# Attention logits: the product with the keys' low half on 64 rows for each map, two maps in two banks, no copy of that low half

## The reference, cut to what matters

```
q = q.reshape(bsz, s, B_HEADS, 2, B_HEAD_DIM) * ATTN_SCALE      # B_HEAD_DIM = 64
k = k.reshape(bsz, s, B_HEADS, 2, B_HEAD_DIM)
...
logits = jnp.einsum('bqhmd,bkhmd->bmhqk', qblk, k).astype(jnp.float32) + bias[None, None]
p = jax.nn.softmax(logits, axis=-1)
attn = p[:, 0] - lam * p[:, 1]
return jnp.einsum('bhqk,bkhd->bqhd', attn.astype(v.dtype), v)
```

## Time and profile before

| | |
|---|---|
| median of 3 runs | 1683.22 us (1682.72 to 1686.58) |
| the profiled execution's own time | 1683.37 us |
| its span in the trace | 1681.6 us |
| granted TensorE clock, mean | 0.999 |
| PE busy | 1673.0 us, 99% of the span |
| DVE, ACT, POOL busy | 1004.9, 832.6 and 805.6 us (60%, 50%, 48%) |

### The profile page before, as it was taken

The page is one execution under the profiler, slowest core; times in us unless marked ns, Lnnn a source line. Parts: engine busy times, 40 slices in busy tenths (PEclk is TensorE's granted clock), DMA queues, the critical chain, the costliest instruction groups (busy, mean ns, idle before and its releaser), DMA issues.

```text
span 1681.6 us, 24045 instructions
## 1 busy us (share of the span) xinstructions
PE 1673.0 (99%) x8873; PEld 1445.6 (86%) x8873; DVE 1004.9 (60%) x1640; ACT 832.6 (50%) x1509; POOL 805.6 (48%) x808
## 2 busy tenths in 40 slices
PE   9999999999999999999999999999999999999998
PEld 7888888888888899988888888888888888999886
DVE  4778876533338967661246788755333489666642
ACT  4676754222245566662255667432223555667322
POOL 3444332433354788854344334334333547888432
PEclk9999999999999999999999999999999999999999
DMA  7422223233333333342352222322342423333422
GB/s 253 136 76 76 76 97 105 75 100 112 129 135 100 101 101 101 102 162 94 97 197 82 94 76 76 101 97 78 100 150 85 142 98 101 101 101 101 163 95 82
DMA packets 147319, 182.77 MB, mean 109 GB/s; under 512 B 3040, under 2 KB 130706, under 8 KB 146194
## 3 DMA queue, kind: packets, MB, share of 16 engines
q1 hardware_dynamic: 147090, 181.35, 32.6%
q10 hardware_dynamic: 128, 0.09, 0.0%
HBM read 170.92 MB, written 10.50 MB: 108 GB/s over the span
## 4 chain that ended last, share of the span: by engine, by line
PE 98%; ACT 0%; DVE 0%; POOL 0%; issue 0%; ACTq 0%; POOLq 0%
PE banks L1852 19%; PE banks L1853 19%; PE banks L1854 19%; PE banks L2088 6%; PE banks L2093 5%; PE banks L2089 5%; PE banks L1887 3%; PE banks L1888 3%; PE banks L1889 3%; PE banks L2167 2%; PE banks L2169 2%; PE banks L2168 2%; PE banks L1916 2%; PE banks L1943 2%; PE banks L2018 1%; PE banks L1927 1%
## 5 line engine op out<-in xcount | busy, mean ns | idle before, releaser
L630 POOL TENSOR_TENSOR w_lo<-raw,w_hi 128x256 fp32r<-128x256 f32 x636 | 514.2, 843 | 784.9 <-ACT w_hi L732 784.9
L1852 PE MATMUL banks<-xg_hi,w_hi 128*128 128x512 f32 x896 | 350.2, 391 | 0.0
L1853 PE MATMUL banks<-xg_lo,w_hi 128*128 128x512 f32 x896 | 349.1, 390 | 0.0
L1854 PE MATMUL banks<-xg_hi,w_lo 128*128 128x512 f32 x896 | 348.7, 389 | 0.0
L1279 DVE TENSOR_TENSOR w_lo<-raw,w_hi 128x768 fp32r<-128x768 f32 (+2 forms) x118 | 100.9, 855 | 175.0 <-ACT w_hi L731 174.8
L1854 PEld LDWEIGHTS banks<-xg_hi,w_lo 128*128 128x128 f32 x896 | 168.2, 188 | 35.5
L1852 PEld LDWEIGHTS banks<-xg_hi,w_hi 128*128 128x128 f32 x896 | 168.4, 188 | 33.8 <-issue 0.2
L1853 PEld LDWEIGHTS banks<-xg_lo,w_hi 128*128 128x128 f32 x896 | 168.4, 188 | 33.5 <-issue 0.2
L731 ACT ACTIVATE w_hi<-raw 128x768 fp32r<-128x768 f32 (+2 forms) x119 | 87.4, 735 | 173.4 <-PE banks L1854 87.9
L732 ACT ACTIVATE w_hi<-raw 128x1280 fp32r<-128x1280 f32 (+3 forms) x119 | 158.8, 1335 | 0.0
L673 POOL TENSOR_TENSOR a_lo<-raw,a_hi 128x1024 fp32r<-128x1024 f32 (+1 forms) x56 | 104.9, 1874 | 40.2 <-ACT a_hi L1042 40.2
(11 more groups left out here) (239 smaller groups left out, 3845.2 us busy)
## 6 DMA issues: line engine op xcount, KB each, us to landing
raw<-in_w_in SPq DMA_DIRECT2D x55, 1024.0 KB, 5.1
raw<-in_w_up SPq DMA_DIRECT2D x44, 1024.0 KB, 5.1
raw<-in_w_br SPq DMA_DIRECT2D x16, 1024.0 KB, 5.0
raw<-in_w_down SPq DMA_DIRECT2D x12, 1024.0 KB, 5.1
x_spill<-x_res SPq DMA_DIRECT2D x4, 2048.0 KB, 7.4
x_res<-x_spill SPq DMA_DIRECT2D x4, 2048.0 KB, 9.5
raw<-in_w_out SPq DMA_DIRECT2D x8, 1024.0 KB, 5.1
raw<-in_w_down SPq DMA_DIRECT2D x8, 896.0 KB, 4.7
```

The lines of the kernel that those rows point to most:

```text
L630: last = nc.gpsimd.tensor_tensor(w_lo[p_][:, k, :], raw[p_][:, k, :], f32(w_hi[p_][:, k, :]), ALU.subtract)
L1852: nc.tensor.matmul(out, w_hi[w][:, k, cols], x_hi[:, a, :], start=first and k == 0, stop=False)
L1853: nc.tensor.matmul(out, w_hi[w][:, k, cols], x_lo[:, a, :], start=False, stop=False)
L1854: mm = nc.tensor.matmul(out, w_lo[w][:, k, cols], x_hi[:, a, :], start=False, stop=last and k == kt - 1)
```

## The change

In `logits` each map has a bank of its own: map m writes columns 0 to 255 of bank 4 + m, for every unit. First come the two products with `k_hi`, on 128 rows as before. Then come two products with `k_lo` on the map's own 64 rows only: the queries' high half by the keys' low half. Map 0 uses rows 0 to 63 and map 1 rows 64 to 127. The product of the queries' low half by the keys' low half is no longer part of the logits.

Since both banks are used by every unit, the logits of unit a now wait until DVE has read those of unit a - 1. DVE reads the two banks' first halves in one instruction.

DVE writes `k_lo` on the map's own rows, so ACT's copy `k_copy` is gone, with its semaphore.

```
             def logits(r, i):
...
-                    pe.wait_ge(k_lo_copy, l * 16 + 4 * r + 2 + i // 2)
...
-                if a >= 2:
-                    pe.wait_ge(biased, l * UNITS + a - 1)
+                if a:
+                    pe.wait_ge(biased, l * UNITS + a)
                 q0 = req * SEQ + qt * P
                 for m in range(2):
-                    for k_part in (k_hi, k_lo):
-                        mm = nc.tensor.matmul(bank[LOGIT + i % 2][:, m * SEQ:(m + 1) * SEQ], q_st[h][:, m, q0:q0 + P],
-                                              k_part[h][:, m, req * SEQ:(req + 1) * SEQ],
-                                              start=k_part is k_hi, stop=k_part is k_lo)
+                    nc.tensor.matmul(bank[LOGIT + m][:, 0:SEQ], q_st[h][:, m, q0:q0 + P],
+                                     k_hi[h][:, m, req * SEQ:(req + 1) * SEQ], start=True, stop=False)
+                for m in range(2):
+                    rows = slice(64 * m, 64 * m + 64)
+                    mm = nc.tensor.matmul(bank[LOGIT + m][:, 0:SEQ], q_st[h][rows, m, q0:q0 + P],
+                                          k_lo[h][rows, m, req * SEQ:(req + 1) * SEQ], start=False, stop=True)
                 mm.then_inc(qk_done, 1)
...
             def softmax_in(r, i):
...
-                    logit[i % 2][:, :, :], bank[LOGIT + i % 2][:, :].rearrange("p (m k) -> p m k", m=2),
+                    logit[i % 2][:, :, :], banks[:, LOGIT:LOGIT + 2, 0:SEQ],
...
             def qk_lo(p, o):
...
-                    last = nc.vector.tensor_tensor(lo[h % 3][other, m, :], t[rows, :], f32(hi[h % 3][rows, m, :]),
-                                                   ALU.subtract)
+                    last = nc.vector.tensor_tensor(lo[h % 3][other if o < 2 else rows, m, :], t[rows, :],
+                                                   f32(hi[h % 3][rows, m, :]), ALU.subtract)
...
-            def k_copy(p, half):
-
-                h = 2 * p + half
-                sc.wait_ge(qk_lo_vector, l * 16 + 4 * p + (turn_of(l, p, 2 + half) + 1))
-                for m in range(2):
-                    rows, other = slice(64 * m, 64 * m + 64), slice(64 - 64 * m, 128 - 64 * m)
-                    last = nc.scalar.activation(k_lo[h % 3][rows, m, :], f32(k_lo[h % 3][other, m, :]), ACT.Copy)
-                last.then_inc(k_lo_copy, 2)
```

More of the change, by code:

```diff
@@ L277, in encoder_kernel @@
     qk_lo_vector = sem("qk_lo_vector")
-    k_lo_copy = sem("k_lo_copy")
     spilled, reloaded = sem("spilled"), sem("reloaded")
@@ L907, in _ @@
                     qk_hi(0, 2 if i == 5 else 0)
[L908 to L911, removed]
                 if i == 5:
@@ L931, in _ @@
                     attention_window(r, i)
-                    if r + 1 < PAIRS and i in (4, 5):
-                        k_copy(r + 1, i - 4)
                     if (l, r, i) == (0, 0, 0):
```

## The result

The changed kernel takes 1702.93 us (median of 4 runs, 1702.43 to 1705.04). The kernel before takes 1682.97 beside it (4 runs). The ratio is 1.0118, 95% interval 1.0106 to 1.0130. So it is slower by 20 us, against 1704 predicted. The profiled execution took 1703.01 us, with a span of 1701.2.

A forecast was written before the change was run, and what follows sets the result against it. The prediction took PE's unbroken stream as the bound: 62 units x 0.28 = 17.4 us, plus 3.1 us of waits at the layers' starts, on 1683.37 gave 1703.9, so 1704 us; range 1685 to 1714.

The forecast's parts named there:

- What bounds the kernel: Whole kernel: PE is one unbroken stream, busy 99% of the span; other engines matter only where PE waits for them.
- ACT's copies at nothing: 32 copies of the keys' low half, 20.2 us of ACT, are gone; hidden behind PE, so they save nothing.
- The wait for `biased`: At each layer's start PE's unit 1 logits wait for DVE's read of unit 0: together 3.1 us.
- The step: PE's stream, each switch between 128-row and narrower matmuls, in or out: 0.20 us each, 0.40 per unit.
- x: Change of one unit's place in PE's stream: two steps less the side-by-side saving, +0.28 us; ends -0.12 and +0.49.
- The pair side by side: The two 64-row `k_lo` matmuls on different row groups overlap, saving one place of 0.12 us (bounds 0 to 0.12).
- Where the step shows: Sign: from second `k_hi` matmul to next half slot about 0.64 instead of 0.36, the pair 0.3 behind that matmul.
- The sum: Whole kernel: 62 units x 0.28 = 17.4, plus 3.1 of waits, on 1683.37 gives 1703.9, predicted as 1704.
- Free steps (2 and 3): Row-mode steps cost PE nothing: 2, no side by side, 1686.5, chance 0.14; 3, side by side, 1679.0, chance 0.16.
- A wait inside the loop (4): PE waits for DVE's read in the loop too: 18 us more if 60 units wait 0.3, chance 0.02.
- x = +0.40: A unit's place in PE's stream, estimated from the skill page's latency and load figures: 1711 in all.
- the clock: PE's granted clock stays at its upper level, 2.4 GHz, and was left out of the sum.

The follow-up runs named there:

- with_copy: Changed kernel with `k_copy`, its semaphore and DVE's old output rows back: 1706.72 us, ratio to before 1.0140.
- full_rows: Changed kernel, but the `k_lo` products use all 128 rows again with ACT's copy back; two banks and wait kept: 1685.96 us, ratio to before 1.0021.
- same_rows: Changed kernel, but both 64-row products use rows 0 to 63, with ACT's copy back: 1711.18 us, ratio to before 1.0175.
- unit1_apart: Changed kernel, but logits of each layer's unit 1 go to banks 6 and 7, needing no wait for unit 0's read: 1704.29 us, ratio to before 1.0120.
- four_steps: Changed kernel, but map by map, each 64-row product between 128-row ones, four steps for a unit instead of two: 1736.74 us, ratio to before 1.0321.
- two_units: Kernel before, but two units' logits issued together: four 128-row products, then four 64-row ones, one step in and out: 1688.09 us, ratio 1.0029.

## Why the prediction was right

- **What bounds the kernel.** Right. PE's stream decided everything: two matmuls less for a unit gave 14.6 us, and outside of the attention parts nothing moved. One reading went too far: PE does wait once for ACT in the kernel before, 0.2 us for `attn_t`, which rows 2, with the two longest waits, don't show. It is not a wait for the copies.
- **ACT's copies at nothing.** Right: layer 0 is equal in with_copy and the changed kernel.
- **The wait for `biased`: 1.2 + 1.9 = 3.1.** Right: 1.12 + 1.92 = 3.04 in full_rows, and nowhere else. Restarting took 0.05 after the read's end and another 0.1 for the load.
- **The step: 0.20 each.** Right: the experiments give 0.19 to 0.20. It came from one place in the trace, the 32-row matmul at the program's start, and from its step out. The step in there was read as 0.30, and taking it would have given x = 0.37 and 1709. Its transpositions ran at half the rate, which was the reason to leave it. That was right, and the reading of the step in was wrong: "0.17 for the load that nothing hides" was the clock. In the changed kernel's profile the same place ran at the upper level (the narrow matmul's two passes, then PE):

```profile
L1758 PE MATMUL banks<-buckets,table x2: 587/588/590, 5.8 to 6.3; 32*8 32x511 f32 x2
...
5.63 0.27 PE L1734 MATMUL banks<-ident,x_tok 128*128 128x128 f32 x1
5.83 1.02 PE L1758 MATMUL banks<-buckets,table 32*8 32x511 f32 x2
```

Both passes last 0.59, and the first starts 0.20 behind the last transposition instead of 0.11. So this step in costs 0.09 and no more. The 0.11 for a load that nothing hides appears only where 128 columns are loaded (the step out, and the `k_lo` pair); `table` has 8. That the width of the load makes the difference is not tested. Using the step out's price for both steps was a choice that the trace of before could not settle, and there is some luck in it.
- **The pair side by side: -0.12.** Right: 0.11 in same_rows. No row of before showed it; the value rested on a bound. The start of both within 0.01 us agrees with the 4 ns of the Trainium skill, "TensorE: Matmul & The Clock Gate", Part 3.
- **Where the step shows.** Not quite as forecast. The prediction wanted 0.64 from the second `k_hi` matmul to the next half slot, with the pair 0.3 behind that matmul. It is 0.52 (111.80 to 112.32) and 0.21. The missing 0.11 lies one place later, in the 0.34 of the half slot's first matmul, because a load that isn't hidden delays the next matmul and not its own start in the trace. The prediction's own working of the step out had it so (0.08 + 0.11); only the sign to look for was put in the wrong stretch.
- **x = +0.28.** 0.277 in unit1_apart, where 64 units pay it without waits.
- **The sum.** Right term by term. 17.4 + 3.1 = 20.5 predicted for the attention parts, 20.23 measured. The profiled execution was 0.9 below the prediction of 1703.9, of which 0.6 is the start of the program.
- **The rivals.** Free steps (2 and 3) are refuted by four_steps. A wait inside the loop (4) didn't come. The smallest lead there is 1.5 us (layer 0, units 2 and 3, a pair that the prediction named), and in the steady part 2.65, where it was 1.8.
- **The page's rule.** The Trainium skill, "TensorEngine Tiling (Array Packing)", section Key Properties, says that a change of tiling mode drains TensorE. This is borne out here as far as the trace can show it: on both sides of a step the load is no longer ahead of its matmul, and the matmul before it holds the stream longer. The estimate from the figures of the Trainium skill, "TensorE: Matmul & The Clock Gate", sections Single matmul latency and LDWEIGHTS, x = +0.40, was 0.12 too high, since the trace shows a step at 0.20 and not at 0.26.

What I did not foresee is the clock: I left it out. It made 3.9 us between two profiled executions at the program's start, and 1.6 us behind layer 1's wait in two of them (with_copy and four_steps). The forecast of 1704 met an execution that had a quick start and no fall.

## What to carry to other kernels

Price a change of the row mode before using 64-row matmuls between 128-row ones. Here a step in and a step out cost 0.39 us of the stream, and a pair on two row groups gives back 0.11, so it would take four pairs (0.39 / 0.11 = 3.5, an estimate that no run here tests) between two steps to gain anything, while the two banks here hold one, or two in the form of two_units. When PE is one stream, look for the one odd matmul that the trace already has; its edges price the new instruction better than durations do, which overlap. Check first at which clock level the place ran, by the steps of the matmuls beside it. A bank that is no longer doubled needs a check of the place where two units stand next to each other, usually the loop's start.

## What the runs showed of the hardware

- A step between 128-row and 64-row matmuls (256 columns, upper clock level) cost 0.19 to 0.20 us in either direction: 0.09 until the next load starts (0.21 instead of 0.12 from 111.80 to 112.01), and the load itself no longer hidden (0.11, in the 0.34 instead of 0.23 from 112.32 to 112.66). With 64-row matmuls on different row groups and different banks, two ran within 0.01 us of each other; on the same row group they were 0.11 apart.
- The granted clock could fall behind a single idle stretch in a stream otherwise without gaps: behind 1.55 us in with_copy and behind 1.05 in four_steps, both in layer 1. Behind 1.55 in the changed kernel, 1.63 in full_rows and 1.44 in same_rows it did not. So the length of the stretch alone doesn't decide it, and what does stays open. Each fall cost 1.6 us.
- At the program's start the same eight matmuls took 2.26 us in one profiled execution and 3.78 in another. The record of the upper level begins at 4.5 us in the first and at 14.5 in the second. The view of windows gives a granted clock of 1.00 for both, since nothing is recorded before; the steps between matmuls show the level there.
